# Seven gate tiles of a fused two-block transformer as split products, and a quarter of a convolution moved to ScalarE and GpSimd

## The chip, the cores and the metric

The kernel runs on one core of a Trainium2 chip. The metric is the device time of one execution in microseconds (us); of the kernel before three runs were taken, with a median of 1699.8 us (1699.54 to 1701.08).

## The reference

Two transformer blocks over 256 tokens of width 1024, all in float32. Only the start of the first block matters here:

```python
h = rms_norm(x, norm1_g)
proj = h @ w_in
a_in, q_c, kv_c, k_rope_in, gates = split_cols(proj, IN_SPLITS)   # 1024, 384, 256, 32, 2048 columns
y_conv = conformer_conv(a_in, ...)     # val * sigmoid(gate), 31-tap depthwise conv, layer norm, silu, w_conv_out
y_mla = mla(q_c, kv_c, k_rope_in, ...) # 8 heads, softmax over 256 keys, w_mla_out
g = sigmoid(gates)
merged = g[..., :1024] * y_conv + g[..., 1024:] * y_mla
x = x + merged @ w_out
```

Behind it come a feed-forward with a 3-tap convolution, a pooling and convolution mixer, a second feed-forward, a sliding-window attention and a mixture of 8 experts. The change touches none of that.

## The kernel before, in words

The program writes out each engine's instructions in order, by hand, with semaphores between the engines; no scheduler moves anything. Activations lie transposed: channels on the 128 partitions, the 256 tokens along the free axis. Weights come from one array `wall` of "granules", 128 x 2048 floats, each of which holds tiles in the order of their use. SyncE loads granule after granule into six buffers `wraw`.

There are two ways to multiply. A **split product** takes float32 apart into a high and a low part: ScalarE copies a granule rounded into `whi` (`split_hi`, line 1293), VectorE writes the rest into `wlo` (`split_next`, line 1703), both with three buffers (`NS`), and TensorE does three products for each tile (`three`, lines 777 to 779). A **whole product** (`whole_job`, line 830) multiplies the unsplit float32 of `wraw`; it needs neither ScalarE nor VectorE. `WHOLE` lists the granules that are not split. In the kernel before these are granules 0 and 1 and everything from the attention's values to the last gate: granules 10 to 19. Gates 9 to 15 are granules 16 (gates 9, 10), 17 (11, 12), 18 (13, 14) and 19 (15); mla_out's two are 20 and 21. `split_hi` of one granule waits until TensorE has used the split granule three places before it.

On TensorE the attention runs head by head: `project` (query and key), `scores`, `flip` (a transposition of the probabilities) and, for two heads at once, `weigh`. Between them stand the whole gates 5 to 15. Each head asks VectorE for `head_in` (drains `qhd`, `khd`), `maxima` and `probabilities`, and ScalarE for `softmax` (two exponentials), `turned` (the copy of a flip, which the next `weigh` and `flip` need) and `weighed` (the high half of a pair's result).

The 31-tap convolution runs on VectorE in the same stretch: four channel tiles, 31 steps each, one `scalar_tensor_tensor` of 128 x 256 per step (`conv`, line 1787), handed out in small counts between the attention's steps, two tiles at a time. When all 124 steps are done, TensorE sums the four tiles over the channels (`sums`, line 869). Then comes a layer norm: VectorE centres (line 1886), ScalarE squares (line 1395), TensorE sums the squares, VectorE takes variance (line 1728) and reciprocal, ScalarE the root in between (`std`, line 1307). ScalarE then takes the sigmoids of gates 5 to 12 (line 1356), the silus (line 1403) and their high halves (line 1408), VectorE the low halves. mla_out's eight tiles follow on TensorE; VectorE drains each (line 1907), the first behind those low halves. conv_out and w_out come next.

GpSimd has no work between the rotary tables (to 34 us) and 180 us.

Of the kernel before, what the change touches and what calls it, by code (L numbers as in the profile page):

```python
# [15 lines left out]
P = 128  # L16
T = 256
# [3 lines left out]
TAPS = 31  # L21
# [158 lines left out]
PLAN = make_plan()  # L180
# [5 lines left out]

WHOLE = [0, 1] + list(range(PLAN.jobs[AT["v1"]][0][0], PLAN.jobs[AT["mla_out"]][0][0]))
SPLITS = [g for g in range(GD) if g not in WHOLE]
# [93 lines left out]
def program(nc, wall, x_d, params_d, consts_d, pos_d, onehot_d, relb_d, poolw_d, recip_d, fgain_d,  # L282
# [6 lines left out]
    with ctx:  # L289
# [11 lines left out]
        def sem(name):  # L301
            return ctx.enter_context(nc.semaphore(name))
# [12 lines left out]
        sq = place("sq", [P, KD, T], f32)  # L315
        v1 = nc.alloc_sbuf_tensor_at("v1", [P, 2, 512], f32, offset=sq_at)
        rstd = place("rstd", [P, T], f32)
        rlat = place("rlat", [P, T], f32)
# [151 lines left out]
        f_act, f_prod, f_tap, f_acc = sem("f_act"), sem("f_prod"), sem("f_tap"), sem("f_acc")  # L470
        vstep, astep = sem("vstep"), sem("astep")
        gate_sig, glu_done, gates_sig = sem("gate_sig"), sem("glu_done"), sem("gates_sig")
# [8 lines left out]
        x_new, biased, pads_set = sem("x_new"), sem("biased"), sem("pads_set")  # L481
        pre_done, z_done, u_copied = sem("pre_done"), sem("z_done"), sem("u_copied")
        pooled_done, pool_mm, yb_done = sem("pooled_done"), sem("pool_mm"), sem("yb_done")
# [112 lines left out]
        def _(pool):  # L596
# [53 lines left out]
            po.tensor_copy(tq[64:96, :], cosb[64:96, :])  # L650
            po.tensor_copy(tq[96:128, :], sinb[96:128, :]).then_inc(rope_ready, 1)
            pool.wait_ge(m_sum, KD)
            pool.dma_start(onehot[:], onehot_d).then_inc(table_loaded, 16)
# [118 lines left out]
        def _(pe):  # L772
# [170 lines left out]
            def gate(j):  # L943
                whole_job(GJ[j], xg1, lambda k: (xg1_done, k + 1))

# [9 lines left out]
            gate(10); weigh(2); flip(6); gate(11); flip(7); gate(12); weigh(3)  # L955
            sums([acc[:, c, :] for c in range(4)], lambda c: (conv_step, 4 * TAPS))
            gate(13)
# [323 lines left out]
        def _(act):  # L1281
# [92 lines left out]
            def weighed(p):  # L1374
                act.wait_ge(pv_done, p + 1)
                sc.activation(oh[:, p, :], bank[6][:, 0:T], ACT.Copy).then_inc(o_hi, 1)
# [3 lines left out]
            for t in range(2):  # L1380
                n = AT["v1"] + t
                wait_job(act, n)
                sc.activation(v1[:, t, :], bank[n % 4], ACT.Copy).then_inc(drained[n % 4], 1)
            softmax(0); softmax(1); turned(0); softmax(2); turned(1); softmax(3)
            weighed(0); turned(2); softmax(4); turned(3); softmax(5)
            weighed(1); turned(4); softmax(6); turned(5); softmax(7)
            weighed(2); turned(6); turned(7); weighed(3)
# [3 lines left out]
            for c in range(4):  # L1391
                act.wait_ge(xc_done, c + 1)
                if c == 0:
                    act.wait_ge(pv_done, 4)
                sc.activation(sq[:, c, :], acc[:, c, :], ACT.Square).then_inc(sq_done, 1)
            split_to(first_mla - 1)
            std()
            for j in range(5, 13):
# [290 lines left out]
        def _(v):  # L1689
# [80 lines left out]
            conv_at = [0]  # L1770

            def conv(count):

                for _ in range(count):
                    m = conv_at[0]
                    if m >= 4 * TAPS:
                        return
                    conv_at[0] += 1
                    pair, rest = divmod(m, 2 * TAPS)
                    tap, c = rest // 2, 2 * pair + rest % 2  # L1780
                    if tap == 0:
                        v.wait_ge(glu_done, c + 1)
                        ve.tensor_scalar(acc[:, c, :], u[:, c, 0:T], pcol("conv_dw_w", c), pcol("conv_dw_b", c),
                                         MUL, ADD).then_inc(conv_step, 1)
                    else:
                        v.wait_ge(conv_step, m - 1)
                        ve.scalar_tensor_tensor(acc[:, c, :], u[:, c, tap:tap + T], pcol("conv_dw_w", 4 * tap + c),  # L1787
                                                acc[:, c, :], MUL, ADD).then_inc(conv_step, 1)
# [80 lines left out]

            conv(8)  # L1870
            for h in range(3):
# [3 lines left out]
            maxima(2); conv(2); head_in(3); probabilities(2); conv(1); head_in(4); conv(2)  # L1875
            maxima(3); conv(2); head_in(5); probabilities(3); conv(2); weighed(0); conv(5); plain_gate(7)
            conv(2); maxima(4); conv(3); probabilities(4); conv(3); plain_gate(8)
            conv(1); maxima(5); conv(2); head_in(6); probabilities(5); conv(2); weighed(1); conv(1); head_in(7)
            conv(2); maxima(6); conv(3); probabilities(6); conv(3); plain_gate(9)
            conv(1); maxima(7); conv(3); probabilities(7); conv(3); plain_gate(10)  # L1880
            conv(2); weighed(2); conv(7); plain_gate(11)
            conv(4 * TAPS); plain_gate(12); weighed(3)
            stats_read[0] += 1
# [575 lines left out]
```

## Time and profile before

| | |
|---|---|
| runs, median (lowest to highest) | 1699.8 us (1699.54 to 1701.08) |
| the profiled execution's own time | 1699.79 us |
| its span, first to last instruction | 1697.8 us |
| TensorE busy | 1669.2 us, 98% |
| VectorE busy | 1410.3 us, 83% |
| ScalarE busy | 1126.3 us, 66% |
| GpSimd busy | 184.7 us, 11% |
| granted TensorE clock, mean | 0.997 |

PE is TensorE's matmuls, DVE is VectorE, ACT ScalarE, POOL GpSimd, SP SyncE. Times are counted from the span's start; L830 is line 830 of the kernel. A group's busy time counts from an instruction's start to its end, and the ends of matmuls in a row overlap, so the distance between starts is the price of one in a row.

### The profile page before, as it was taken

How to read it: one execution, taken by the hardware profiler on the slowest of the kernel's cores; microseconds unless marked ns; L12 is line 12 of the kernel's file. 1: busy time of each engine (PE TensorE's matmuls, PEld its weight loads, DVE VectorE, ACT ScalarE, POOL GpSimd, SP SyncE). 2: the span in 40 equal slices, each digit the busy share in tenths (PEclk: the TensorE clock that was granted, in tenths of full speed). 3: DMA queues.
4: the chain of work that ended last, by engine and by line, in shares of the span. 5: the costliest groups of instructions: out<-in, count | busy, mean ns of one | idle time of the engine just before them, and what ended most of it. 6: DMA issues, size and time to landing. Idle time of an engine off the chain costs nothing.

```text
span 1697.8 us, 26295 instructions
## 1 busy us (share of the span) xinstructions
PE 1669.2 (98%) x10142; PEld 1474.5 (87%) x10142; DVE 1410.3 (83%) x1391; ACT 1126.3 (66%) x1128; POOL 184.7 (11%) x166
## 2 busy tenths in 40 slices
PE   9999999999999999999999999999999999999997
PEld 8888999999999998888888888888888888888876
DVE  7997799858876657788888888888888888888888
ACT  5325587753544446677777777777777777777776
POOL 5000355423400011020000000000000000000120
PEclk9999999999999999999999999999999999999999
DMA  8335498694455555469999999999999999999995
GB/s 335 124 124 199 158 412 312 197 279 154 180 192 198 199 198 157 151 252 422 395 380 386 369 384 389 364 390 382 367 386 392 371 385 381 380 384 359 380 385 247
DMA packets 76909, 513.51 MB, mean 302 GB/s; under 512 B 9536, under 2 KB 10016, under 8 KB 18720
## 3 DMA queue, kind: packets, MB, share of 16 engines
q1 hardware_dynamic: 70128, 487.14, 74.0%
q0 software_dynamic: 6560, 25.32, 5.5%
q8 instruction: 52, 0.85, 0.2%
q14 instruction: 25, 0.20, 0.0%
q10 hardware_dynamic: 144, 0.00, 0.0%
HBM read 488.27 MB, written 24.15 MB: 302 GB/s over the span
## 4 chain that ended last, share of the span: by engine, by line
PE 86%; DVE 8%; ACT 3%; DMA 2%; issue 1%; SPq 0%; DVEq 0%; ACTq 0%
PE psum L777 26%; PE psum L779 26%; PE psum L778 26%; PE psum L830 3%; DVE wlo L1703 3%; DMA wraw<-weights 2%; PE psum L1215 1%; DVE acc L1787 1%; ACT whi L1293 1%; PE psum L1183 0%; PE psum L917 0%; ACT s L1518 0%; PE psum L869 0%; DVE zc L2008 0%; PE psum L1073 0%
## 5 line engine op out<-in xcount | busy, mean ns | idle before, releaser
L1703 DVE TENSOR_TENSOR wlo<-wraw,whi 128x2048 fp32r<-128x2048 f32 (+1 forms) x445 | 1012.3, 2275 | 190.4 <-ACT whi L1632 106.9
L1632 ACT ACTIVATE whi<-wraw 128x2048 fp32r<-128x2048 f32 x336 | 645.2, 1920 | 223.4 <-PE psum L779 214.3
L777 PE MATMUL psum<-whi,xgh 128*128 128x512 f32 x896 | 354.0, 395 | 1.5 <-DVE xgl L1703 0.9
L779 PE MATMUL psum<-whi,xgl 128*128 128x512 f32 x896 | 349.9, 391 | 0.0
L778 PE MATMUL psum<-wlo,xgh 128*128 128x512 f32 x896 | 348.8, 389 | 0.0
L777 PE MATMUL psum<-ah,whi 128*128 128x256 f32 x1048 | 292.7, 279 | 2.1 <-DVE u L1793 1.3
L778 PE MATMUL psum<-al,whi 128*128 128x256 f32 x1048 | 289.9, 277 | 0.0
L779 PE MATMUL psum<-ah,wlo 128*128 128x256 f32 x1048 | 289.9, 277 | 0.0
L1293 ACT ACTIVATE whi<-wraw 128x2048 fp32r<-128x2048 f32 x104 | 198.9, 1913 | 108.1 <-PE psum L779 104.0
L777 PEld LDWEIGHTS psum<-ah,whi 128*128 128x128 f32 x1048 | 196.9, 188 | 4.4 <-DVE u L1793 1.9
L779 PEld LDWEIGHTS psum<-whi,xgl 128*128 128x128 f32 x896 | 168.1, 188 | 36.0
L777 PEld LDWEIGHTS psum<-whi,xgh 128*128 128x128 f32 x896 | 168.2, 188 | 35.8 <-issue 1.1
L778 PEld LDWEIGHTS psum<-wlo,xgh 128*128 128x128 f32 x896 | 168.4, 188 | 33.9
L778 PEld LDWEIGHTS psum<-al,whi 128*128 128x128 f32 x1048 | 196.8, 188 | 0.2
L779 PEld LDWEIGHTS psum<-ah,wlo 128*128 128x128 f32 x1048 | 197.0, 188 | 0.0
L777 PE MATMUL psum<-whi,ath 128*128 128x512 f32 x448 | 175.9, 393 | 0.1
L779 PE MATMUL psum<-whi,atl 128*128 128x512 f32 x448 | 174.6, 390 | 0.0
L778 PE MATMUL psum<-wlo,ath 128*128 128x512 f32 x448 | 174.4, 389 | 0.0
L761 POOL DMA_INDIRECT xtm<-expert_outs,idx x4 | 10.5, 2636 | 854.2 <-issue 845.8
L779 PEld LDWEIGHTS psum<-whi,atl 128*128 128x128 f32 x448 | 84.1, 188 | 17.7
L777 PEld LDWEIGHTS psum<-whi,ath 128*128 128x128 f32 x448 | 84.1, 188 | 17.5 <-issue 0.5
L778 PEld LDWEIGHTS psum<-wlo,ath 128*128 128x128 f32 x448 | 84.2, 188 | 17.0
(345 smaller groups left out, 2174.4 us busy)
## 6 DMA issues: line engine op xcount, KB each, us to landing
wraw<-weights SPq DMA_DIRECT2D x453, 1024.0 KB, 4.9
expert_rows<-zeros POOLq DMA_DIRECT2D x1, 8704.0 KB, 51.3
expert_outs<-zeros POOLq DMA_DIRECT2D x1, 4608.0 KB, 71.2
expert_outs<-ysb SPq DMA_DIRECT2D x8, 512.0 KB, 6.7
xgt<-expert_rows SPq DMA_DIRECT2D x8, 512.0 KB, 5.7
bias_rows<-ttab POOLq DMA_DIRECT2D x1, 3072.0 KB, 36.0
btab<-bias_rows POOLq DMA_DIRECT2D x4, 384.0 KB, 7.6
xres<-x SPq DMA_DIRECT2D x1, 1024.0 KB, 5.0
```

The costliest lines, as they stand in the source:

```text
L761: pool.indirect_dma_start(out=xtm[:, t, :], out_offset=None, in_=rows_out, in_offset=bass.IndirectOffsetOnAxis(ap=idx[:, i:i + 1], axis=0) ...
L777: nc.tensor.matmul(out, lh, rh, start=start, stop=False)
L778: nc.tensor.matmul(out, lh, rl, start=False, stop=False)
L779: return nc.tensor.matmul(out, ll, rh, start=False, stop=stop)
L830: mm = nc.tensor.matmul(jb(n), wraw[:, g % NW, off:off + P], x[:, k, :], start=(k == 0), stop=(k == PLAN.jobs[n][-1][2]))
L1215: mm = nc.tensor.transpose(bank[6][:, i * P:(i + 1) * P], act_[:, i * P:(i + 1) * P], ident)
L1293: sc.activation(whi[:, i % NS, :], wraw[:, g % NW, :], ACT.Copy).then_inc(hi_done, 1)
L1632: sc.activation(whi[:, (GS + j) % NS, :], wraw[:, g % NW, :], ACT.Copy).then_inc(hi_done, 1)
L1703: return ve.tensor_tensor(dst, value, hi.bitcast(f32), SUB)
L1787: ve.scalar_tensor_tensor(acc[:, c, :], u[:, c, tap:tap + T], pcol("conv_dw_w", 4 * tap + c), acc[:, c, :], MUL, ADD).then_inc(conv_step, 1)
```

## The change

Three things, all between 77 and 165 us:

1. `WHOLE` ends before gate 9: granules 16 to 19 are split. Gates 9 to 15 become `job` (split products with the split activations `ah`, `al`) on TensorE. ScalarE gets three `split_hi` between the heads, VectorE three `split_next`; granule 19 and mla_out's first granule are split behind the last pair of heads. The layer norm's root stands ahead of the split of mla_out's second granule.
2. The convolution's channel tile 3 leaves VectorE. ScalarE makes one product per tap into a ring of four buffers `tapped` (the first one, with the bias, straight into `acc`), GpSimd adds 30 of them up. The tap counts on ScalarE stand ahead of the exponentials and copies, the last eight behind the last head's exponentials. VectorE keeps 93 steps, in a new order.
3. VectorE does two steps ahead of the first head where it did eight.

```diff
-WHOLE = [0, 1] + list(range(PLAN.jobs[AT["v1"]][0][0], PLAN.jobs[AT["mla_out"]][0][0]))
+LATE_GATES = 9
+WHOLE = [0, 1] + list(range(PLAN.jobs[AT["v1"]][0][0], PLAN.jobs[GJ[LATE_GATES]][0][0]))
...
+        tapped = nc.alloc_sbuf_tensor_at("tapped", [P, 4, T], f32, offset=sq_at + 4 * T * 4)
...
+            for tap in range(1, TAPS):
+                pool.wait_ge(tap_made, tap + 1)
+                if tap > 1:
+                    pool.wait_ge(tap_added, tap - 1)
+                add(acc[:, 3, :], acc[:, 3, :], tapped[:, tap % 4, :], tap_added)
             pool.wait_ge(m_sum, KD)
...
             def gate(j):
-                whole_job(GJ[j], xg1, lambda k: (xg1_done, k + 1))
+                if j < LATE_GATES:
+                    whole_job(GJ[j], xg1, lambda k: (xg1_done, k + 1))
+                else:
+                    job(GJ[j], ah, al)
...
-            sums([acc[:, c, :] for c in range(4)], lambda c: (conv_step, 4 * TAPS))
+            sums([acc[:, c, :] for c in range(4)], lambda c: (conv_step, 3 * TAPS) if c < 3 else (tap_added, TAPS - 1))
...
-            softmax(0); softmax(1); turned(0); softmax(2); turned(1); softmax(3)
-            weighed(0); turned(2); softmax(4); turned(3); softmax(5)
-            weighed(1); turned(4); softmax(6); turned(5); softmax(7)
+            tap_at = [0]
+
+            def taps(count):
+
+                for tap in range(tap_at[0], min(tap_at[0] + count, TAPS)):
+                    if tap == 0:
+                        act.wait_ge(glu_done, 4)
+                        sc.activation(acc[:, 3, :], u[:, 3, 0:T], ACT.Identity, scale=pcol("conv_dw_w", 3),
+                                      bias=pcol("conv_dw_b", 3)).then_inc(tap_made, 1)
+                    else:
+                        if tap > 4:
+                            act.wait_ge(tap_added, tap - 4)
+                        sc.activation(tapped[:, tap % 4, :], u[:, 3, tap:tap + T], ACT.Copy,
+                                      scale=pcol("conv_dw_w", 4 * tap + 3)).then_inc(tap_made, 1)
+                    tap_at[0] = tap + 1
+
+            taps(4); softmax(0); taps(3); softmax(1); taps(2); turned(0); softmax(2); taps(2); turned(1); taps(1); softmax(3)
+            taps(2); weighed(0); turned(2); split_hi(); softmax(4); taps(3); turned(3); softmax(5); split_hi()
+            weighed(1); turned(4); taps(3); softmax(6); split_hi(); turned(5); taps(3); softmax(7)
+            taps(TAPS)
             weighed(2); turned(6); turned(7); weighed(3)
...
+            std()
             split_to(first_mla - 1)
-            std()
...
+            ORDER = [(c, tap) for tap in range(3) for c in range(2)]
+            for step in range(TAPS - 3):
+                ORDER += [(0, step + 3), (1, step + 3), (2, step)]
+            ORDER += [(2, tap) for tap in range(TAPS - 3, TAPS)]
...
-            conv(8)
+            conv(2)
...
-            maxima(3); conv(2); head_in(5); probabilities(3); conv(2); weighed(0); conv(5); plain_gate(7)
-            conv(2); maxima(4); conv(3); probabilities(4); conv(3); plain_gate(8)
-            conv(1); maxima(5); conv(2); head_in(6); probabilities(5); conv(2); weighed(1); conv(1); head_in(7)
-            conv(2); maxima(6); conv(3); probabilities(6); conv(3); plain_gate(9)
-            conv(1); maxima(7); conv(3); probabilities(7); conv(3); plain_gate(10)
-            conv(2); weighed(2); conv(7); plain_gate(11)
-            conv(4 * TAPS); plain_gate(12); weighed(3)
+            maxima(3); conv(2); head_in(5); probabilities(3); conv(2); weighed(0); plain_gate(7)
+            split_next(); conv(2); maxima(4); conv(3); probabilities(4); conv(3); plain_gate(8)
+            conv(1); maxima(5); conv(2); head_in(6); probabilities(5); split_next(); weighed(1); head_in(7)
+            conv(1); maxima(6); conv(3); probabilities(6); plain_gate(9); split_next()
+            maxima(7); conv(1); probabilities(7); plain_gate(10)
+            weighed(2); conv(2); plain_gate(11)
+            conv(3 * TAPS); plain_gate(12); weighed(3)
```

How the instructions stand, at three places. In these rows a line number is that of the kernel it comes from; names are tiles (out<-in).

ScalarE, from the exponentials of head 6 to the squares of the layer norm, in the kernel before:

```order
L1363 ACTIVATE prob,st<-psum,st 128x256 x2
L1371 ACTIVATE probT<-psum 128x512
L1363 ACTIVATE prob,st<-psum,st 128x256 x2
L1376 ACTIVATE oh<-psum 128x256
L1371 ACTIVATE probT<-psum 128x512 x2
L1376 ACTIVATE oh<-psum 128x256
L1293 ACTIVATE whi<-wraw 128x2048
L1395 ACTIVATE sq<-acc 128x256 x4
```

The same place with the change:

```order
L1374 ACTIVATE prob,st<-psum,st 128x256 x2
L1304 ACTIVATE whi<-wraw 128x2048
L1382 ACTIVATE probT<-psum 128x512
L1407 ACTIVATE tapped<-u,par 128x256 x3
L1374 ACTIVATE prob,st<-psum,st 128x256 x2
L1407 ACTIVATE tapped<-u,par 128x256 x8
L1387 ACTIVATE oh<-psum 128x256
L1382 ACTIVATE probT<-psum 128x512 x2
L1387 ACTIVATE oh<-psum 128x256
L1304 ACTIVATE whi<-wraw 128x2048 x2
L1423 ACTIVATE sq<-acc 128x256 x4
```

Ahead of the copy `probT` of flip 5 there is now a weight split, ahead of that of flip 6 the last eight products, and ahead of the squares two splits.

ScalarE, from those squares to the high halves of the normed convolution, before:

```order
L1395 ACTIVATE sq<-acc 128x256 x4
L1293 ACTIVATE whi<-wraw 128x2048
L1307 ACT_TABLE_LOAD
L1307 ACTIVATE var<-var 128x256
L1356 ACT_TABLE_LOAD
L1356 ACTIVATE gates<-gates 128x256 x8
```

With the change:

```order
L1423 ACTIVATE sq<-acc 128x256 x4
L1318 ACT_TABLE_LOAD
L1318 ACTIVATE var<-var 128x256
L1304 ACTIVATE whi<-wraw 128x2048
L1367 ACT_TABLE_LOAD
L1367 ACTIVATE gates<-gates 128x256 x8
```

The split of mla_out's second granule stood ahead of the root and stands behind it.

VectorE, from the low half of the first pair of heads to the maxima of head 4, before:

```order
L1703 TENSOR_TENSOR ol<-psum,oh 128x256
L1787 SCALAR_TENSOR_TENSOR acc<-u,par,acc 128x256 x5
L1793 TENSOR_TENSOR gates<-psum,rstd 128x256
L1787 SCALAR_TENSOR_TENSOR acc<-u,par,acc 128x256 x2
L1844 TENSOR_REDUCE st<-psum 128x2
```

With the change:

```order
L1731 TENSOR_TENSOR ol<-psum,oh 128x256
L1826 TENSOR_TENSOR gates<-psum,rstd 128x256
L1731 TENSOR_TENSOR wlo<-wraw,whi 128x2048
L1820 SCALAR_TENSOR_TENSOR acc<-u,par,acc 128x256 x2
L1877 TENSOR_REDUCE st<-psum 128x2
```

Five convolution steps ahead of gate 7's drain are gone, and a low split stands ahead of the maxima (`TENSOR_REDUCE`) of head 4.

## Rows read from the trace of the kernel before

**Rows 1.** Page, part 1: engine, busy us and share, instructions.

```profile
PE 1669.2 (98%) x10142; PEld 1474.5 (87%) x10142; DVE 1410.3 (83%) x1391; ACT 1126.3 (66%) x1128; POOL 184.7 (11%) x166
```

**Rows 2.** Chain that ended last, 60 to 200 us: start, us, engine, tile, line.

```profile
82.24 2.43 PE psum L830 x10
...
103.39 3.65 PE psum L830 x16
...
138.11 1.92 PE psum L869 x8
...
145.25 0.43 DVE var L1728
...
156.94 0.42 DVE gates L1907
```

**Rows 3.** Timeline of TensorE at the first heads: start, us, what, [idle before].

```profile
76.54 4.48 PE L830 MATMUL psum<-lat,wraw 128*128 128x256 f32 x20
82.24 1.56 PE L830 MATMUL psum<-lat,wraw 128*128 128x256 f32 x6 [1.23 <-DVE qhd L1837]
```

**Rows 4.** Timeline of TensorE from 80 to 185 us.

```profile
106.88 0.60 PE L927 MATMUL psum<-con,prob 128*128 128x128 f32 x4
...
115.19 1.08 PE L939 MATMUL psum<-probT,v 128*64 128x256 f32 x8
...
129.58 3.62 PE L830 MATMUL psum<-xg,wraw 128*128 128x256 f32 x16
133.04 0.60 PE L927 MATMUL psum<-con,prob 128*128 128x128 f32 x4
...
164.15 0.28 PE L777 MATMUL psum<-lnh,whi 128*128 128x256 f32 x1
...
169.59 0.28 PE L777 MATMUL psum<-lnh,whi 128*128 128x256 f32 x1
```

**Rows 5.** Timeline of VectorE from 30 to 170 us.

```profile
77.42 4.43 DVE L1787 SCALAR_TENSOR_TENSOR acc<-u,par,acc 128x256 f32<-128x256 f32 x11
...
108.39 0.69 DVE L1844 TENSOR_REDUCE st<-psum 128x2 f32<-128x512 f32 x1
...
110.57 0.61 DVE L1854 TENSOR_SCALAR prob<-prob,st 128x256 f32<-128x256 f32 x2
...
114.74 0.42 DVE L1837 TENSOR_TENSOR qhd<-psum,tq 128x256 f32<-128x256 f32 x1
...
141.63 2.29 DVE L1703 TENSOR_TENSOR wlo<-wraw,whi 128x2048 fp32r<-128x2048 f32 x1
```

**Rows 6.** Timeline of ScalarE from 30 to 170 us.

```profile
107.52 0.60 ACT L1371 ACTIVATE probT<-psum 128x512 f32<-128x512 f32 x1 [3.69 <-PE psum L927]
...
109.31 0.47 ACT L1363 ACTIVATE prob<-psum,st 128x256 f32<-128x256 f32 x1 [1.20 <-DVE st L1847]
...
138.44 1.90 ACT L1293 ACTIVATE whi<-wraw 128x2048 fp32r<-128x2048 f32 x1
```

**Rows 7.** Timeline of ScalarE in the first feed-forward: a product with a column.

```profile
212.52 0.49 ACT L1449 ACTIVATE fside<-fpad,par 128x256 f32<-128x256 f32 x1
```

**Rows 8.** Timeline of GpSimd: sums of 128 x 256 in three places.

```profile
8.65 5.35 POOL L601 TENSOR_TENSOR ssum<-ssum,sq 128x256 f32<-128x256 f32 x6
...
18.07 2.48 POOL L639 TENSOR_TENSOR ang<-ang 128x256 f32<-128x256 f32 x1
...
227.74 2.84 POOL L601 TENSOR_TENSOR facc<-facc,fside 128x256 f32<-128x256 f32 x2 [2.34 <-ACT fside L1449]
```

**Rows 9.** Timeline of VectorE beside the first of these.

```profile
8.57 6.24 DVE L1745 SCALAR_TENSOR_TENSOR al<-xres,par,ah 128x256 fp32r<-128x256 f32 x8
```

**Rows 10.** Stretches: length, busy us by engine, granted clock, DMA share, GB/s.

```profile
177.00:180.00 3.00, 1.25 (x6) 0.84 (x6) 2.90 (x9) 0.89 (x3) 0.00 (x0) 1.00 0.69 235
180.00:182.00 2.00, 1.70 (x8) 1.54 (x9) 0.67 (x2) 2.00 (x2) 1.34 (x2) 0.71 0.52 205
182.00:184.00 2.00, 2.00 (x11) 2.00 (x11) 1.80 (x1) 0.16 (x1) 0.00 (x0) 0.50 0.01 1
```

More of the change, by code:

```diff
@@ L470, in program @@
         f_act, f_prod, f_tap, f_acc = sem("f_act"), sem("f_prod"), sem("f_tap"), sem("f_acc")
-        vstep, astep = sem("vstep"), sem("astep")
+        vstep = sem("vstep")
+        tap_made, tap_added = sem("tap_made"), sem("tap_added")
         gate_sig, glu_done, gates_sig = sem("gate_sig"), sem("glu_done"), sem("gates_sig")
@@ L481, in program @@
         x_new, biased, pads_set = sem("x_new"), sem("biased"), sem("pads_set")
-        pre_done, z_done, u_copied = sem("pre_done"), sem("z_done"), sem("u_copied")
+        u_copied = sem("u_copied")
         pooled_done, pool_mm, yb_done = sem("pooled_done"), sem("pool_mm"), sem("yb_done")
@@ L1770, in _ @@
             conv_at = [0]
+            ORDER = [(c, tap) for tap in range(3) for c in range(2)]
+            for step in range(TAPS - 3):
+                ORDER += [(0, step + 3), (1, step + 3), (2, step)]
+            ORDER += [(2, tap) for tap in range(TAPS - 3, TAPS)]
+            PLACE = {x: m for m, x in enumerate(ORDER)}
             def conv(count):
@@ L1775, in conv @@
                     m = conv_at[0]
-                    if m >= 4 * TAPS:
+                    if m >= 3 * TAPS:
                         return
                     conv_at[0] += 1
-                    pair, rest = divmod(m, 2 * TAPS)
-                    tap, c = rest // 2, 2 * pair + rest % 2
+                    c, tap = ORDER[m]
                     if tap == 0:
@@ L1785, in conv @@
                     else:
-                        v.wait_ge(conv_step, m - 1)
+                        v.wait_ge(conv_step, PLACE[c, tap - 1] + 1)
                         ve.scalar_tensor_tensor(acc[:, c, :], u[:, c, tap:tap + T], pcol("conv_dw_w", 4 * tap + c),
```

## The prediction

> **What bounds the kernel now.** I read the page's busy table first: TensorE is busy 98% of the span, so time is gained only where TensorE does less or waits less [rows 1]. I then read the chain of waits from 60 to 200 us, where the gate tiles and the first attention lie [rows 2]. The reader is to see there which engine carries the end at each moment. From 82 to 145 us it is TensorE, without a wait: it starts the third head's projection at 82.24, runs gate 7 from 103.39, and the sums over the convolution from 138.11 to 140.03. At 145.25 the chain leaves TensorE: VectorE takes the variance, ScalarE works up to the silus, VectorE drains the first mla_out tile at 156.94 and goes on without TensorE up to w_out. So a TensorE saving counts in full only until 140; behind it the time is set by how soon after the sums VectorE reaches that first mla_out tile, 16.9 us now (156.94 less 140.03). Since the work behind it is unchanged, whatever moves this instant moves the end.
>
> **What is saved.** A whole gate takes 3.46 us (129.58 to 133.04); a split one is 24 products, and 48 of them go from 164.15 to 169.59, so 2.72 [rows 4]. That is 0.74 a gate, 5.2 for seven, but only gates 9 to 12 lie ahead of the sums: **-2.9**. The other three lie where TensorE is not the bound. Ahead of the first head VectorE now does 2 convolution steps where it did 8; a step is 0.40 (4.43 for 11) [rows 5], so 2.4 us less. TensorE waited 1.23 us there for qhd; the two projections before it, 20 matmuls from 76.54, end near 80.85, so the third can start there, not at 82.24 [rows 3]: **-1.4**. Past that the head start is VectorE's slack and worth nothing.
>
> VectorE is relieved of 31 steps, 12.3 us, and gets four low splits at 2.2 each [rows 5], 8.8 in all: less work, but each split is a wait for ScalarE, and that decides.
>
> **What is added ahead of the sums.** I count from the end of gate 7, which is the start of the third flip, 106.88 now; weigh 1 stands at 115.19, 8.3 later [rows 4]. In the new order ScalarE's first gate split stands behind that flip's copy: flip 0.43, copy 0.6, split 1.85, hand-overs 0.2 [rows 4, 6], so VectorE, which waits for it, starts its low split at 3.1, ends at 5.3, does 2 steps (0.8) and the maxima of head 4 (0.69 and a small instruction, 0.8) [rows 5] and is at 6.9. ScalarE's two exponentials, 0.47 each with a short read behind it [rows 6], take an estimated 1.0, then come 3 products, then the copy of flip 3, which weigh 1 needs. A product is like the 0.49 of the side tap [rows 7], about 0.35 to 0.4 apart. That copy ends at 9.7 or 9.8, so weigh 1 waits **1.5** where it did not wait.
>
> VectorE goes on with three steps, the probabilities (0.61 and a small instruction, 0.75), three steps, a drain (0.34), a step and the maxima of head 5: 11.6. ScalarE's exponentials end at 12.7, its second split at 14.6; VectorE, at 13.8 by two steps, a head's two inputs (0.42 each, 0.66 in a row) and the probabilities [rows 5], waits for it. Its low split ends at 16.85, a low half and the inputs of head 7 at 17.85; TensorE, by weigh, projection, flip, scores, gate 9 and flip at 17.6, waits some **0.35** for them before scores 7. A step and the maxima of head 6 end at 19.05, ScalarE's exponentials at 20.15, the third split, which stands next, at 22.0, and only then the copy that weigh 2 needs, at 22.6; TensorE is there at 21.6: **1.15**. VectorE waits for that third split too, so the maxima of head 7 end at 25.05, the exponentials at 26.15. Behind them stand the last eight products, and behind those the copy of flip 6. Product 27 on needs its buffer free, that is GpSimd's sum of four taps back. The sums follow each other every 0.89 us (5.35 for 6), and none runs during a split on VectorE (one took 2.48 beside one) [rows 8]. So sums 20 to 26 run from 24.25 to 30.1, the last product ends at 30.6, the copy at 31.55; TensorE stood ready for flip 7 at 26.95: **4.7**. Flip, gate 12, weigh 3 and the sums end at 37.7, against 33.0 now (140.03 less 107.04) [rows 2]. GpSimd's last sum is done some 3 us ahead of its use, so it costs nothing, but with the eight products out of the way it would be the next to be late.
>
> **Behind the sums.** The last gate's split and mla_out's first are now both left until weigh 3, so ScalarE's four squares end about 3.5 us behind the sums; gate 13 (2.7) covers this. VectorE's way to the variance is four centrings (1.4 with 0.2 to start), two low splits (4.4) and a drain (0.3): 6.3 us behind the sums, where it is 5.2 now (145.25 less 140.03), **+1.1**. On ScalarE the square root now stands ahead of mla_out's second split. That split needs a slot which gate 14 frees, 7.3 behind the sums (2.7, squares like the 1.92 of the sums, 2.7), just when ScalarE comes to it; it lies between root and sigmoids, on the path, **+1.9** [rows 2, 6]. The sigmoids, a split, the silus and their copies follow as before. So VectorE comes to the first mla_out tile 19.9 us behind the sums, not 16.9, and TensorE, through its gates sooner, stands some 4.5 us before mla_out's fifth tile.
>
> **Two unknown prices.** First, GpSimd beside VectorE. While six chained sums ran on GpSimd, eight VectorE instructions with two SBUF inputs took 6.24 us, 0.77 each [rows 8, 9], against 0.40 for a step of that kind alone [rows 5]. So each of the 30 sums can take 0.37 from VectorE if a step runs beside it. The Trainium skill says so as a rule (GPSIMD Engine Reference, Key points): GpSimd shares its SBUF interfaces with VectorE and contends with instructions that have two SBUF inputs. The rows bear this out; without the rule and the row the sum would be 1.4 lower. Lower bound 0, if the sums fall on PSUM work and waits. Upper: some 13 sums fall ahead of gate 7, where 2 us of VectorE idling and the head start absorb all but 1.4, and some 4 of those behind it on steps in the chain, 1.4: 2.8. I take 1.4, as a third of VectorE's time there is steps, so not every sum meets one. Second, the clock. TensorE, idle more than half of 177 to 180, was granted 0.71 of its clock from 180 to 182 and 0.50 (1.2 GHz) from 182 to 184 [rows 10]: of these 4 us 0.58 and 1.0 are lost, 1.6. Two stalls over 4 us may each bring this: 0 to 3.2; a stall's loss counts only where TensorE bounds next, which is gate 12 behind the first. I take 1.0.
>
> **Sum.** -1.4 - 2.9 + (1.5 + 0.35 + 1.15 + 4.7 = 7.7) + 1.1 + 1.9 = +6.4, and with 1.4 and 1.0, **+8.8 us**. On the profiled execution's 1699.79 (1697.8 span and 2.0 around it), which stands at the median of 1699.8, this is **1708.6**. The ends of the unknowns give 1706.2 to 1712.2.
>
> The added DMA work is none: the same loads are issued, and SyncE's refill behind gates 9 to 15 is released by the low split instead of the matmul, earlier. The removed semaphores cost nothing.
>
> **Rivals.** *A: the path stays with TensorE.* If VectorE comes through with less delay than I walk, none of the stalls ahead of the sums shows, and with the tail shorter too the saving comes through: 1699.8 - 1.4 - 5.2 = 1693.2. For it speaks that VectorE has 3.5 us less to do; against it, that the waits come from the order on ScalarE, not from VectorE's load. It decides if the copy of flip 3 is done within 8.3 us of gate 7. Chance 0.12. *B: only the eight products are harmless.* If GpSimd has its sums done so early that the last products never wait for a buffer, the 4.7 goes; -4.3 + 3.0 + 3.0 = +1.7, or 1701.5, and with one half-priced unknown up to 1703. Chance 0.17. *C: GpSimd is slower still.* Its sums beside the feed-forward took 1.42 each (2.84 for 2) [rows 8]; five more in the pacing at 0.53 each are 2.7, and with the upper unknowns it is 1709 to 1715. Chance 0.16. My forecast has 0.55.
>
> **How the numbers follow.** A measurement of this kernel tells 0.2% (3.4 us) from nothing. Faster: A, 0.12. Same (1696.4 to 1703.2): B, and a little less to allow for its upper end, 0.16. Slower: the rest, 0.72. The range goes from B's low edge, 1701, to 1713, leaving out A and the upper half of C.
>
> **What would show it.** Right: in the chain, ScalarE's product line and GpSimd's sums ahead of the last flip; on TensorE a wait of 4 to 5 us before flip 7 and one like it within mla_out; VectorE's first mla_out drain near 20 us behind the sums; steps on VectorE above 0.40 beside sums; a granted clock of 0.5 behind a stall. Wrong: TensorE without waits from 82 to 140, or the sums ending before 139.

## The result, and the profile after

| | before | changed |
|---|---|---|
| runs, median (lowest to highest) | 1699.94 us (1699.54 to 1701.08, 4 runs) | 1715.48 us (1713.52 to 1716.74, 4 runs) |
| the profiled execution's own time, its span | 1699.79, 1697.8 us | 1714.25, 1712.4 us |
| TensorE busy | 1669.2 us | 1668.5 us |
| granted clock, mean | 0.997 | 0.994 |

The ratio is 1.0083, with a 95% interval of 1.0065 to 1.01, which is 11 to 17 us: slower, as forecast, but by 15.5 us as medians where 8.8 were forecast, and outside the range.

The page's busy table after the change, against [rows 1]:

```profile
PE 1668.5 (97%) x10198; PEld 1476.0 (86%) x10198; DVE 1415.7 (83%) x1364; ACT 1145.1 (67%) x1163; POOL 209.5 (12%) x196
```

VectorE has 27 instructions less (31 steps of 0.40 us gone, four splits of 2.2 new), which should save it 3.5 us, and is busy 5.4 us *longer* [rows 1, 5]: its instructions have become slower by 8.9 in all. GpSimd has its 30 sums, 25.2 us.

The chain that ended last, where [rows 2] had TensorE alone (start, us, engine, tile, line):

```profile
108.60 1.91 ACT whi L1304
110.52 0.02 issue
110.54 2.29 DVE wlo L1731
...
115.48 1.19 ACT tapped L1407 x3
...
117.21 1.08 PE psum L947 x8
...
129.28 1.81 ACT whi L1304
131.09 0.02 issue
131.12 2.29 DVE wlo L1731
...
135.27 1.60 ACT tapped L1407 x4
136.87 0.04 issue
136.91 0.73 POOL acc L604
...
137.78 0.73 POOL acc L604
...
138.65 0.73 POOL acc L604
...
140.18 0.49 ACT probT L1382
140.68 0.14 issue
140.81 1.09 PE psum L935 x4
```

The gate splits between the heads on ScalarE (whi) and VectorE (wlo) lie on the path, then the products (tapped), then GpSimd's sums one by one, and only behind them the copy (probT) of flip 6, which the last flip needs. The sums over the convolution begin at 147.43 in this chain and end at 149.36, where they began at 138.11 [rows 2].

TensorE's timeline, its waits in brackets, against [rows 3, 4]:

```profile
76.70 6.64 PE L838 MATMUL psum<-lat,wraw 128*128 128x256 f32 x30
...
97.43 1.13 PE L838 MATMUL psum<-lat,wraw 128*128 128x256 f32 x4 [0.70 <-DVE gates L1826]
...
99.68 1.13 PE L925 MATMUL psum<-khd,qhd 128*128 128x256 f32 x4 [0.68 <-DVE khd L1872]
...
107.47 0.60 PE L935 MATMUL psum<-con,prob 128*128 128x128 f32 x4
...
117.21 1.08 PE L947 MATMUL psum<-probT,v 128*64 128x256 f32 x8 [1.36 <-ACT probT L1382]
...
122.00 1.13 PE L925 MATMUL psum<-khd,qhd 128*128 128x256 f32 x4 [0.91 <-DVE khd L1872]
...
126.73 1.13 PE L925 MATMUL psum<-khd,qhd 128*128 128x256 f32 x4 [0.33 <-DVE khd L1872]
...
131.62 1.08 PE L947 MATMUL psum<-probT,v 128*64 128x256 f32 x8 [0.94 <-ACT probT L1382]
...
140.81 1.09 PE L935 MATMUL psum<-con,prob 128*128 128x128 f32 x4 [4.78 <-ACT probT L1382]
...
169.87 0.58 PE L785 MATMUL psum<-oh,whi 128*128 128x256 f32 x1 [4.40 <-DVE gates L1940]
```

The third head's projection now follows without a wait (30 matmuls in one row), so the head start is there. But the third flip, 107.47, is 0.6 later than before (106.88): two waits for VectorE (0.70 and 0.68) and what restarting behind them costs have eaten the 1.4 and more. Then come the waits that the prediction walked through: 1.36, 0.33, 0.94 and 4.78, and 4.40 within mla_out. The 0.91 is one that it did not have.

VectorE's timeline, three convolution steps beside GpSimd's sums and three without, the normalising pair, and the way to the first mla_out drain:

```profile
80.22 2.58 DVE L1820 SCALAR_TENSOR_TENSOR acc<-u,par,acc 128x256 f32<-128x256 f32 x3
...
83.39 1.26 DVE L1820 SCALAR_TENSOR_TENSOR acc<-u,par,acc 128x256 f32<-128x256 f32 x3
...
88.60 1.12 DVE L1887 TENSOR_SCALAR prob<-prob,st 128x256 f32<-128x256 f32 x2
...
168.05 1.43 DVE L1731 TENSOR_TENSOR lnl<-acc,lnh 128x256 fp32r<-128x256 f32 x4 [5.31 <-ACT lnh L1436]
169.40 0.41 DVE L1940 TENSOR_TENSOR gates<-psum,gates 128x256 f32<-128x256 f32 x1
```

Three steps take 2.58 us instead of 1.26, and the pair 1.12 instead of 0.61 [rows 5]. The first drain of mla_out, at 169.40, stands 20.0 us behind the end of the sums (149.36), behind a wait of 5.31 for ScalarE.

The stretches around the two long waits (columns as in [rows 10]):

```profile
138.00:140.00 2.00, 0.00 (x0) 0.00 (x0) 0.00 (x0) 1.28 (x4) 1.71 (x3) 0.69 0.00 0
140.00:142.00 2.00, 1.19 (x6) 1.22 (x7) 1.75 (x3) 0.73 (x3) 1.69 (x3) 0.50 0.00 0
142.00:144.00 2.00, 2.00 (x11) 2.00 (x11) 0.59 (x2) 0.54 (x1) 0.73 (x1) 0.50 0.00 0
...
170.00:172.00 2.00, 2.00 (x10) 2.00 (x11) 2.00 (x2) 1.99 (x5) 0.00 (x0) 0.50 0.00 0
```

Behind each the granted clock is 0.50 (1.2 GHz). Flip 7 and gate 12 run in the first: 18 of the gate's 24 products come 0.21 us apart instead of 0.113, so from flip 7 to weigh 3 it is 5.54 us.

### The profile page after: what moved, and what is told of

Read it like the earlier page. It is cut to its first block, busy times and chain, and to the rows that moved or that the text cites. A ratio compares the mean times of both kernels' runs of the same rounds, so it can differ in the third digit from the quotient of the medians.

```text
span 1712.4 us, 26450 instructions
## 1 busy us (share of the span) xinstructions
PE 1668.5 (97%) x10198; PEld 1476.0 (86%) x10198; DVE 1415.7 (83%) x1364; ACT 1145.1 (67%) x1163; POOL 209.5 (12%) x196
## 4 chain that ended last, share of the span: by engine, by line
PE 83%; DVE 9%; ACT 4%; DMA 2%; issue 1%; SPq 0%; POOL 0%; DVEq 0%; ACTq 0%; POOLq 0%
PE psum L785 27%; PE psum L787 26%; PE psum L786 26%; DVE wlo L1731 3%; DVE acc L1820 2%; DMA wraw<-weights 2%; ACT whi L1304 1%; PE psum L1226 1%; PE psum L838 0%; PE psum L1194 0%; ACT s L1546 0%; PE psum L877 0%; DVE zc L2041 0%; PE psum L1084 0%; ACT whi L1660 0%
## 5 line engine op out<-in xcount | busy, mean ns | idle before, releaser
L785 PE MATMUL psum<-ah,whi 128*128 128x256 f32 x1104 | 309.9, 281 | 3.5 <-DVE u L1826 1.8
L786 PE MATMUL psum<-al,whi 128*128 128x256 f32 x1104 | 306.1, 277 | 0.0
L787 PE MATMUL psum<-ah,wlo 128*128 128x256 f32 x1104 | 306.0, 277 | 0.0
L785 PEld LDWEIGHTS psum<-ah,whi 128*128 128x128 f32 x1104 | 208.4, 189 | 6.0 <-DVE u L1826 2.4
L786 PEld LDWEIGHTS psum<-al,whi 128*128 128x128 f32 x1104 | 208.2, 189 | 0.3
L787 PEld LDWEIGHTS psum<-ah,wlo 128*128 128x128 f32 x1104 | 208.2, 189 | 0.0
L787 PEld LDWEIGHTS psum<-whi,xgl 128*128 128x128 f32 x896 | 168.2, 188 | 36.2
L786 PEld LDWEIGHTS psum<-wlo,ath 128*128 128x128 f32 x448 | 84.2, 188 | 16.9
```

The source lines that it names most:

```text
L785: nc.tensor.matmul(out, lh, rh, start=start, stop=False)
L786: nc.tensor.matmul(out, lh, rl, start=False, stop=False)
L787: return nc.tensor.matmul(out, ll, rh, start=False, stop=stop)
```

## The experiments

Two stretches of TensorE are compared in all kernels, since they leave out most of what single executions add elsewhere: from the values' first matmul (v1) to the sums over the convolution, and from v1 to the first product of up1 (the first feed-forward), past which no kernel differs. Each is one execution. The first four kernels came to v1 some 2.8 us later than the others, by a wait of 3.4 to 3.7 us that ends near 44 us, ahead of every change, and the kernel before took 1703.5 beside them, so the whole times that their expectations name are to be read 3.7 higher; the ratios are each against the kernel before in the same set.

| kernel | v1 to sums | waits in it | v1 to up1 | ratio of whole runs (95%) |
|---|---|---|---|---|
| before | 65.0 us | 1.2 | 129.0 us | |
| changed | 74.2 | 9.7 | 141.5 | 1.0083 (1.0065 to 1.01) |
| conv tile moved only | 65.5 | 1.4 | 129.9 | 1.0004 (0.9992 to 1.0017) |
| gates split only | 68.4 | 5.4 | 135.3 | 1.0054 (1.0029 to 1.0079) |
| head start only | 63.5 | 0 | 126.1 | 0.9996 (0.9973 to 1.002) |
| products early | 69.5 | 6.9 | 137.4 | 1.0048 (1.003 to 1.0066) |
| changed, no sums | 68.4 | 5.4 | 135.3 | 1.0033 (1.0018 to 1.0049) |
| products early, no sums | 63.6 | 2.1 | 130.8 | 1.0017 (0.9998 to 1.0035) |
| products early, four gates | 68.1 | 5.9 | 130.4 | 1.0029 (1.0011 to 1.0047) |
| changed, filler | 72.0 | 5.6 | 139.6 | 1.0074 (1.0052 to 1.0096) |
| changed, drains first | 73.5 | 9.8 | 137.2 | 1.0045 (1.0028 to 1.0061) |
| head start, drains first | 63.6 | 0 | 124.6 | 0.9981 (0.9967 to 0.9994) |
| the same, last three gates split | 63.6 | 0 | 128.4 | 0.9998 (0.9981 to 1.0015) |
| before, 30 idle sums | 72.1 | 5.9 | 135.9 | 1.004 (1.0025 to 1.0055) |

One thing in the second stretch can't be put down to the kernels. In six of the traces (before, changed, conv tile moved, products early, filler, idle sums) the clock falls to half within w_out, as [rows 10] shows it for the kernel before; there conv_out and w_out take 37.6 to 38.3 us together, and where the clock stays whole and TensorE has no longer wait, 36.2. Between a kernel of these six and one of the others the column "v1 to up1" is off by 1.3 to 2.1 us. With the same 2.5 us of waits ahead of it the clock fell in the kernel before and stayed whole in gates split only; no run here tells why.

**The parts alone.** The convolution's move alone is the changed kernel with all gates whole, the splits in the order of before:

```diff
-LATE_GATES = 9
+LATE_GATES = 16
```

> Gates 9 to 15 whole again; the convolution's fourth tile stays on ScalarE and GpSimd, 2 steps ahead of the first head. Theory (order on ScalarE): without splits the maxima of head 7 come 7 us earlier, the last eight products are done before TensorE needs the copy of flip 6, no wait before flip 7 above 0.5 us; the head start of 1.4 us is kept or eaten by GpSimd's contention: 1698.5 to 1701. Rival (GpSimd beside VectorE is the loss): its 3 us or more stay, 1703 or above.

The split gates alone are the kernel before with gates 9 to 15 split, and their splits where the change puts them:

```diff
+                if j < LATE_GATES:
                     whole_job(GJ[j], xg1, lambda k: (xg1_done, k + 1))
+                else:
+                    job(GJ[j], ah, al)
```

> Gates 9 to 15 split, the whole convolution on VectorE, 8 steps ahead of the first head as before. Theory: the waits for the splits ahead of weigh 1 and weigh 2 (1.4 and 1 us) are there without any GpSimd work; VectorE has 6.6 us of low splits and some 4 us of waits for ScalarE more, so the sums stand near 143.5 instead of 138, and the way from the sums to mla_out's first drain is 20 us instead of 16.9: 1708 to 1710. Rival (the loss is all in GpSimd's share): 1700 or below, since the gates are shorter.

The head start alone is the kernel before with fewer steps ahead of the heads:

```diff
-            conv(8)
+            conv(2)
```

> The kernel before with 2 convolution steps instead of 8 ahead of the first head, nothing else. Theory: TensorE's wait of 1.2 us before the third projection goes, nothing takes its place before the sums, as VectorE idles 4 us before them: 1698.4. Rival: VectorE comes later with everything behind, the sums stay where they are: 1699.8.

The head start alone makes the first stretch 1.5 us shorter: the -1.4 holds. With the convolution's tile moved as well it is 0.5 *longer* than before, although VectorE has 31 steps less: some 1.9 us of the head start go to GpSimd. The gates alone, without a product or a sum, cost 3.3 us ahead of the sums and 6.3 up to up1 (7.9 without the half clock within w_out that only the kernel before has), so their order on ScalarE and VectorE is a loss by itself. Of the two waits that were expected for them, the one ahead of weigh 2 is there (1.06); ahead of weigh 1 it is only 0.17, so the changed kernel's 1.36 there is mostly the three products ahead of the copy. Each part apart is cheaper than the two together (0.5 and 3.3 against 9.2).

**Products early.** ScalarE's products go four at a time from the first softmax on, and none stands behind softmax 7.

```diff
-            weighed(1); turned(4); taps(3); softmax(6); split_hi(); turned(5); taps(3); softmax(7)
-            taps(TAPS)
+            weighed(1); turned(4); taps(TAPS); softmax(6); split_hi(); turned(5); softmax(7)
```

> The change with the 31 products handed out four at a time, the last ahead of the exponentials of head 6; nothing else moved. Theory: the 4.8 us before flip 7 and the half clock behind it (2.4 us on gate 12) go, no other wait grows above 1 us: 1707 to 1709. Rival (GpSimd's contention with VectorE sets the time): the sums stay near 147, 1713 to 1716.

The wait at flip 7 is gone and no half clock follows there: the eight last products were worth 4.7 us. The others stay or grow (2.4 in two waits within projections, 2.3 in three ahead of scores, 1.1 ahead of weigh 1 and 1.0 ahead of weigh 2), so the theory's "no other wait grows above 1 us" failed; and 4.5 remain within mla_out.

**GpSimd's sums left out**, of the changed kernel and of the one with early products; the fourth tile then holds its first tap alone.

```diff
-                add(acc[:, 3, :], acc[:, 3, :], tapped[:, tap % 4, :], tap_added)
+                pool.sem_inc(tap_added, 1)
```

> The changed kernel with GpSimd's 30 sums left out: GpSimd only counts the products on, so the convolution's fourth channel tile holds its first tap alone; order, waits and ScalarE's products are kept. Told as the stretch from the values' first matmul to the sums over the convolution on TensorE: 65.0 us in the kernel before, 74.2 in the changed one. Theory (GpSimd's adds take some 3.3 us from VectorE ahead of the last flip, and the last eight products alone, at 0.37, hold flip 7 for about 3.2 of its 4.8 us): the stretch is near 69 (74.2 less 3.3 less 1.6), or 67 if the shorter stall leaves the clock whole; VectorE's steps stand at 0.40 and the normalising pair at 0.62 throughout. Rival 1 (the adds cost VectorE nothing that counts, only the pacing does): 72.6. Rival 2 (GpSimd's pace is the whole of the stall at flip 7): that wait is under 1 us and the stretch is near 65 to 66. Whole kernel, by the theory 5 to 7 us below the changed one.

> The kernel with the products early (the fourth of the first four) with GpSimd's 30 sums left out in the same way. No product stands ahead of the last flips here, so only VectorE's contention is taken away. The same stretch is 69.5 us with the sums. Theory (contention is worth 3 to 3.5 us and shows as the waits for khd and for the gate drains): 66.0 to 66.5, with TensorE's waits of 2.4 ahead of a projection and 2.3 ahead of scores down to under 1 each, while weigh 2 still waits 1 to 2 for the third split. Rival (those waits come from ScalarE's products, which stand ahead of the exponentials, and not from the adds): 69 to 69.5 as before. Whole kernel, by the theory some 3 us below the one with the sums.

In the changed kernel it is 5.8 us less. TensorE's timeline without the sums:

```profile
105.50 0.60 PE L935 MATMUL psum<-con,prob 128*128 128x128 f32 x4
...
115.24 1.08 PE L947 MATMUL psum<-probT,v 128*64 128x256 f32 x8 [1.36 <-ACT probT L1382]
...
127.84 1.08 PE L947 MATMUL psum<-probT,v 128*64 128x256 f32 x8 [0.67 <-ACT probT L1382]
...
135.57 1.09 PE L935 MATMUL psum<-con,prob 128*128 128x128 f32 x4 [3.32 <-ACT probT L1382]
```

The third flip comes 1.9 earlier, counted from v1, the waits for khd (0.91 and 0.33) are gone, weigh 2 waits 0.27 less: 3.4 us of contention ahead of flip 7. The wait at flip 7 falls from 4.78 to 3.32 only, so ScalarE's products make two thirds of it, and GpSimd's pace one third. Rivals 1 and 2 both fall. With early products the price is even 5.9 us, and my 3 to 3.5 was too low; but there too nothing is won against the kernel before, since 4.4 us of wait within mla_out remain.

**Sums that nobody needs.** To the kernel before, 30 chained sums on spare memory are added from the first maxima on.

```diff
+            pool.wait_ge(rope_ready, 1)
+            pool.wait_ge(neg_done, 1)
+            pool.memset(tapped[:], 0.0).then_inc(tap_added, 1)
+            for tap in range(1, TAPS):
+                pool.wait_ge(tap_added, tap)
+                add(tapped[:, 0, :], tapped[:, 0, :], tapped[:, 1, :], tap_added)
```

> The kernel before, its whole convolution on VectorE, with 30 chained GpSimd sums of two 128x256 tiles added, from the first head's maxima on. They work on spare memory and no engine needs a result of theirs ahead of the sums over the convolution; nothing else changes. Theory (each sum takes about 0.37 us from VectorE where it meets a step or a normalising pair, which fill some 21 of 30 us there): 30 x 0.37 x 0.7 = 7.8 us less than 3 of VectorE's idle time, so from the values' first matmul to the sums about 70 us (69 to 73), where the kernel before has 65.0; steps of 0.7 to 0.86 us on VectorE in that time and waits of TensorE for qhd, khd and the gate drains. Rival 1 (the price that the prediction took, 1.4 for 30 sums): 66 to 66.7. Rival 2 (GpSimd yields: its sums stretch and VectorE keeps 0.40 a step): under 65.5.

VectorE's groups from 89 to 115 us, before and with the sums (busy us, mean ns of one, behind the bar):

```profile
L1787 DVE SCALAR_TENSOR_TENSOR acc<-u,par,acc 128x256 f32<-128x256 f32 x33 | 14.2, 477 | 0.0
...
L1854 DVE TENSOR_SCALAR prob<-prob,st 128x256 f32<-128x256 f32 x10 | 3.1, 350 | 0.2
```

```profile
L1796 DVE SCALAR_TENSOR_TENSOR acc<-u,par,acc 128x256 f32<-128x256 f32 x17 | 13.8, 850 | 0.0
L1863 DVE TENSOR_SCALAR prob<-prob,st 128x256 f32<-128x256 f32 x8 | 6.1, 798 | 0.1
```

In the same time VectorE does 17 steps instead of 33. That is 17 x 0.37 + 8 x 0.45 = 9.9 us in these two groups, or 0.33 for each sum. TensorE pays 7.0 of them, 4.7 as waits (one of 3.71 for a gate drain) and about 1.7 as half clock behind that wait (0.77 and 0.80 granted from 100 to 108). The theory holds, and both rivals fall. GpSimd does not yield: from the first start to the last end its 30 sums took 25.4 us, 0.85 each.

**The last three gates whole**, in the kernel with early products; the third split ahead of the sums goes (its two lines are left out here), and behind them it is the order of before.

```diff
-LATE_GATES = 9
+LATE_GATES = range(9, 13)
...
-            std()
             split_to(first_mla - 1)
+            std()
```

> The kernel with the products early, but only gate tiles 9 to 12 as split products; 13 to 15 whole, and behind the sums ScalarE and VectorE in the order of the kernel before. Theory (the third split costs ahead of the sums, the last gates' split and the root's place cost behind them): the wait ahead of weigh 2, 2.1 us, falls under 0.7, so the stretch from the values' first matmul to the sums goes from 69.5 to about 67.5; from the end of the sums to VectorE's first drain of mla_out it is 16.9 to 17.4 us as in the kernel before, not 20; the wait within mla_out of 4.5 us goes to under 1.5. The end of the span, from the values' first matmul, stands 3 to 4 us behind the kernel before, where the seven gates made it 8.6. Rival (the last three gates as split products are worth their 2.2 us on TensorE, and the way behind the sums is set by the load of mla_out's weights): the end stays at 8 to 10.

Gates 13 to 15 as split products, with their splits and the root's place, cost 7 us up to up1 (137.4 to 130.4; 5.3 without the half clock within w_out), and not 2.2 to the good. Ahead of the sums weigh 2 does not wait, but the 1.1 ahead of weigh 1 stays, and the stretch is 68.1, not 67.5. Behind them the first drain is back at 16.9 us (143.0 to 159.9), the wait within mla_out at 0.76, and without the long wait no half clock follows. What remains to the kernel before is ahead of the sums. The rival falls.

**Filler.** 36 products into an unread bank stand where TensorE waits for flip 7.

```diff
+            for m in range(36):
+                nc.tensor.matmul(bank[4][:, 0:T], ah[:, m % KD, 0:P], ah[:, m % KD, :], start=True, stop=True)
             flip(7); gate(12); weigh(3)
```

> The changed kernel with 36 products of the operand with itself put on TensorE between gate 11 and the last flip, into a bank that nobody reads: some 4.1 us of work in which TensorE would wait 4.8. Nothing is computed from them; nothing else moves. Theory (the stall halves the granted clock, and gate 12 pays 2.4 us for it): gate 12 runs at 0.113 us a product, the stretch from the values' first matmul to the sums over the convolution is 71.8 us and not 74.2, and the end of the span comes 2 to 2.6 us earlier, 1713 against 1715.5 as medians. Rival 1 (the half clock falls on time that TensorE waits away again behind the sums): the sums come 2.4 earlier and the end within 0.7 of the changed kernel. Rival 2 (the clock falls for another reason than the stall): gate 12 stays at 0.21 us a product and the end is unchanged or later.

The stretches of that kernel around flip 7:

```profile
136.00:140.00 4.00, 4.00 (x34) 3.84 (x33) 0.25 (x2) 2.88 (x8) 3.43 (x5) 1.00 0.28 119
140.00:144.00 4.00, 3.48 (x31) 3.34 (x32) 2.37 (x5) 1.02 (x2) 2.21 (x4) 1.00 0.01 4
```

The clock stays at 1.00 and gate 12 at 0.113 a product: the stall had halved it, and that cost 2.2 us at the sums, 1.9 of which are there at up1. As far as up1 both rivals fall. The whole runs can't tell it (1.0074 against 1.0083, intervals of 0.002): this execution lost it again in the first feed-forward, whose second matrix product took 62.2 us instead of 60.1 at a granted clock of 1.00.

**Drains first.** On VectorE the four lnl, which wait for ScalarE's silus, come behind mla_out's third drain; once in the changed kernel, once with the head start in the kernel before.

```diff
-            lows(4, lnl, lambda c: acc[:, c, :], lnh, (ln_hi, 0), ln_lo)
             for i in range(KD):
...
+                if i == 2:
+                    lows(4, lnl, lambda c: acc[:, c, :], lnh, (ln_hi, 0), ln_lo)
```

> The changed kernel with one move on VectorE: the four low halves of the normalised convolution (lnl), which wait for ScalarE's silus, come behind the third drain of mla_out instead of ahead of the first. Theory (the finished mla_out tiles wait behind lnl in VectorE's queue, so the way from the sums to the first drain, 20.2 us, is that queue and not work): the first drain comes at the end of its tile, about 3 us earlier, TensorE's wait of 4.4 us within mla_out falls under 1 and no half clock follows near 168 to 172; from the values' first matmul to the first product of up1 it is 137.0 to 138.5 us, where the changed kernel has 141.5 and the kernel before 129.0. Whole kernel 1711 to 1712.5. Rival (mla_out's drains wait for the sigmoids or for a split as well): the wait moves to the next drain or to conv_out, and the gain is under 1.5.

> The kernel before with two convolution steps instead of eight ahead of the first heads (the part that came out as worth 1.4 us) and with lnl behind mla_out's third drain. No gate is split and no product moved. Theory: TensorE has no wait from the values to the sums, and its 0.9 us within mla_out go too; from the values' first matmul to up1 125.0 to 126.0 us, where the kernel before has 129.0 and the head start alone 126.1; whole kernel 2 to 4 us below the kernel before (ratio 0.998 to 0.999). Rival (behind the sums the chain to w_out is VectorE's, and what is saved at mla_out is waited for at w_out): no better than the head start alone, 1.4 below.

In the changed kernel TensorE no longer waits within mla_out, and up to up1 it is 4.3 us less. Not all of that is the move's: 0.7 lie ahead of the sums, where the clock came back sooner behind flip 7 in this execution, and 1.4 are the half clock within w_out that this execution does not have; some 2 are left, less than the 3 to 4.5 of the theory. The rival has a part too: a wait of 2.84 appears ahead of conv_out:

```profile
175.11 0.58 PE L785 MATMUL psum<-lnh,whi 128*128 128x256 f32 x1 [2.84 <-DVE gates L1939]
```

With the head start, nothing else of the change, it is the fastest kernel: 1698.24 us against 1701.23, ratio 0.9981 (0.9967 to 0.9994). Up to up1 it is 4.4 us less, of which 1.6 is again the half clock within w_out, 1.5 the head start, and 1.3 come within mla_out, where the wait is gone. The head start alone does not have these 1.3, but whole runs can't tell the two kernels apart, since their intervals overlap. VectorE now drains as the tiles end:

```profile
152.46 0.42 DVE L1906 TENSOR_TENSOR gates<-psum,gates 128x256 f32<-128x256 f32 x1 [0.95 <-PE psum L779]
...
155.67 1.42 DVE L1703 TENSOR_TENSOR lnl<-acc,lnh 128x256 fp32r<-128x256 f32 x4
```

**The last three gates on top of that**, with the root ahead of mla_out's second half.

```diff
+LATE_GATES = 13
...
-            conv(4 * TAPS); plain_gate(12); weighed(3)
+            conv(4 * TAPS); split_next(); plain_gate(12); weighed(3)
```

> The same kernel with gate tiles 13 to 15 as split products: the first of their two low halves on VectorE between the last convolution step and the drain of gate 12, the second behind the centring; ScalarE's halves behind the last softmax and the last flip's copy, the root ahead of mla_out's second half as in the changed kernel. Theory (behind the sums TensorE bounds once the drains no longer stand behind lnl): three gates at 0.74 are 2.2 us less on TensorE, of which at least half comes through: from the values' first matmul to up1 123 to 125 us, whole kernel 3 to 6 us below the kernel before. Rival (VectorE's two further splits, 4.5 us, push its chain to mla_out's first drain past the tile's end, as in the changed kernel): TensorE waits 2 us or more within mla_out or w_out, and the kernel is no faster than without them, or slower.

The rival holds, though the lack is more ScalarE's than VectorE's:

```profile
162.43 2.29 DVE L1707 TENSOR_TENSOR wlo<-wraw,whi 128x2048 fp32r<-128x2048 f32 x1 [2.97 <-ACT whi L1297]
```

VectorE's second low split puts the variance 1.1 us later behind the sums (8.3 from their start, where the kernel without it has 7.2). ScalarE's chain of root, split, sigmoids, silus and copies is then longer by one split (1.9), the split behind it is late, VectorE waits 2.97 and TensorE 2.84 ahead of conv_out, at half clock afterwards. Up to up1 that is 3.8 us more (128.4 to 124.6): what TensorE saves there it waits away, and more.

## Why the prediction was right in sign and too low

| step | forecast | measured |
|---|---|---|
| head start | -1.4 | -1.5 |
| four split gates | -2.9 | about -2 |
| waits ahead of the sums | 7.7 | 7.4 (1.36, 0.33, 0.94, 4.78) |
| way behind the sums | +3.0 | +3.1 to the first drain (20.0 less 16.9) |
| GpSimd beside VectorE | 1.4 (0 to 2.8) | 3.4 |
| half clock | 1.0 (0 to 3.2) | 2.2 at flip 7 and gate 12 |
| sum | +8.8 | +12.6 by these, +12.5 up to up1 |

In the last column the wait of 0.33 and 0.27 of the 0.94 stand twice, in the waits and in GpSimd's 3.4; counted once, the sum is 12.0, and 0.5 are not accounted for.

**What held.** The four waits come where the walk put them, each within 0.25 us, with the releasers that it named, and the one within mla_out as well: the order on ScalarE decides. Rival A (no wait) and rival B (the eight products harmless) are out.

**What failed** is the step "Two unknown prices". For GpSimd the mechanism was right and the size was not: "I take 1.4, as a third of VectorE's time there is steps" measured 3.4, over my upper bound of 2.8. Two things went into that. I took it that idle time and the head start absorb what falls ahead of gate 7, all but 1.4, and halved that again; the third flip is 1.9 us sooner without the sums, most of it the waits of 0.70 and 0.68. And I charged only the steps with two inputs; the normalising pair, which reads one tile, goes from 0.61 to 1.12 beside the sums. For the clock I took 1.0 of a possible 3.2; flip 7 and gate 12 alone paid 2.2, because the flip and three quarters of the gate ran at the half clock on the path. In these terms 2.0 and 1.2 us were missing.

**A smaller miss** is the 2.72 of a split gate, taken from tiles that follow each other. Between flips the second product starts up to 0.30 behind the first, and gate 9 takes 3.0 us (122.78 to 125.80), so four gates give about 2 and not 2.9. The kernel with early products and no sums says the same: 63.6 us less its 2.1 of waits is some 2 us under the 63.5 of the head start alone. The miss on the other side is small. Rival C named the right cause, a dearer GpSimd, but priced it at the pacing of the last sums, which was right at 4.8 as it stood.

**What it put at nothing** is the work behind: "Since the work behind it is unchanged, whatever moves this instant moves the end." Up to up1 the change costs 12.5 us, which would have made 1712.3 and lies inside the range; the rest carries the median out of it. Behind up1 the two kernels do the same, yet the profiled executions part by another 1.9 us by their ends, and the medians by 3. Half clock does not make the 1.9, since both executions have one such stretch near 440 us; it comes in pieces, 0.7 up to 464 us of the kernel before and 0.9 near 1634. The same work took 1495.8 to 1500.8 us in the fourteen traces, 1497.8 in the changed kernel's, so the 1.9 lies within what single executions differ by. That the change causes any of it is not shown, and with four runs the ratio's interval holds 12.5 as well.

## What to carry to other kernels

Work moved off a full VectorE to GpSimd is not free for VectorE: count every short SBUF-to-SBUF instruction that it meets, of one input or two, at twice its time (0.85 for 0.48 and 0.80 for 0.35 here). A low split of 2.29 us that was running first kept its 2.29, and the sum that met it was the one to stretch (1.96 for 0.73). A step put ahead of a short copy on an idle engine (here ScalarE's products, splits and the copies that flips wait for) costs TensorE what of its length lies past TensorE's arrival (1.36, 0.94 and 4.78 here), however idle that engine is on the page. Look in each queue for a waiting instruction ahead of ready ones: moving four of them behind three drains, together with fewer convolution steps ahead of the first head, beat the kernel before by 0.2%, and needed none of the new work.

## What was not expected of the hardware

- Beside a chain of GpSimd sums, VectorE's short instructions go about one for one with them, 0.85 us a pair; alone a step is 0.40, and a sum in the changed kernel, while VectorE is idle, 0.73. The Trainium skill (SBUF — State Buffer, "SBUF: two separate sides") calls the shared pair of ports an exclusive lock held for the whole instruction. By that a pair would take an estimated 1.13 (0.40 and 0.73); the measured 0.85 is less. Some of the 0.73 may lie outside the lock, but no run here shows it.
- The normalising pair's slowing agrees with the same section's other case, a VectorE instruction in a 2-port mode, though no run here shows which mode it ran in.
- At a granted clock of 1.00 the second matrix product of the first feed-forward took 60.1 us in one execution and 62.2 in another; no run here tells why.
